# First pair's key norm moved up a tile, six low parts given to GpSimd, the first gates' sigmoid ahead of a copy

## The reference, cut to what matters

```python
z = h @ w_in                                        # h = rmsnorm(x)
kk = heads(kf * k_k)                                # k is a slice of z
kk = kk / maximum(sqrt(sum(kk * kk, -1)), 1e-12)    # the key norm
S = S * w_t + (S @ -kk) (kk * a)^T + v k^T          # the scan over tokens
y = (groupnorm(y) + bonus) * g
g_a, g_b = split(sigmoid(z_gate + gate_b), 2)
x = x + (g_a * (y @ w_proj_a) + g_b * (attn @ w_proj_b)) @ w_out
x = x + conv_ffn(rmsnorm(x))
```

## Time and profile before

| | |
|---|---|
| median of 3 runs | 1123.92 us (1123.31 to 1125.4) |
| the profiled execution, its own time | 1125.01 us |
| its span (first to last instruction) | 1123.0 us |
| PE busy | 1095.9 us, 98% of the span |
| DVE busy | 687.6 us, 61% |
| ACT busy | 503.7 us, 45% |
| POOL busy | 92.8 us, 8% |
| PE share of the chain that ended last | 88%; DVE 7%, ACT 1% |
| granted TensorE clock | 0.999 |

### The profile page before, as it was taken

The page is one execution under the profiler, slowest core; times in us unless marked ns, Lnnn a source line. Parts: engine busy times, 40 slices in busy tenths (PEclk is TensorE's granted clock), DMA queues, the critical chain, the costliest instruction groups (busy, mean ns, idle before and its releaser), DMA issues.

```text
span 1123.0 us, 17984 instructions
## 1 busy us (share of the span) xinstructions
PE 1095.9 (98%) x6760; PEld 864.9 (77%) x6760; DVE 687.6 (61%) x1163; ACT 503.7 (45%) x865; POOL 92.8 (8%) x145
## 2 busy tenths in 40 slices
PE   7999999989999999999999999999999999999997
PEld 6887888767777777777766888888888888888886
DVE  4224566678878777787785444547776777752224
ACT  6426555633524445253533333455556555641122
POOL 8100001101010110101110100100000000000000
PEclk9999999999999999999999999999999999999999
DMA  8632333210111111111312544333332333232221
GB/s 212 131 94 76 94 95 94 76 39 20 39 39 48 39 57 57 48 58 39 113 57 86 153 137 131 123 103 103 93 95 83 105 93 97 86 105 94 94 75 75
DMA packets 154390, 97.01 MB, mean 86 GB/s; under 512 B 30761, under 2 KB 143575, under 8 KB 154327
## 3 DMA queue, kind: packets, MB, share of 16 engines
q1 hardware_dynamic: 148800, 79.72, 24.5%
q0 software_dynamic: 5376, 16.37, 4.6%
q10 hardware_dynamic: 151, 0.04, 0.0%
HBM read 87.71 MB, written 8.39 MB: 86 GB/s over the span
## 4 chain that ended last, share of the span: by engine, by line
PE 88%; DVE 7%; ACT 1%; DMA 1%; issue 1%; SPq 1%; DVEq 0%; ACTq 0%
PE ps L1607 15%; PE ps L1610 15%; PE ps L1609 15%; PE ps L1590 5%; PE ps L2086 4%; PE ps L2087 4%; PE ps L2085 4%; PE ps L1592 4%; PE ps L1591 4%; PE ps L1734 3%; PE ps L1884 2%; PE ps L1863 1%; PE ps L1688 1%; PE ps L1819 1%; PE ps L1682 1%; DMA raw<-in_w_in 1%
## 5 line engine op out<-in xcount | busy, mean ns | idle before, releaser
L1096 DVE TENSOR_TENSOR wlo<-raw,whi 128x1024 fp32r<-128x1024 f32 x142 | 173.5, 1222 | 214.2 <-ACT whi L691 141.7
L691 ACT ACTIVATE whi<-raw 128x1024 fp32r<-128x1024 f32 x124 | 131.1, 1057 | 133.1 <-PE ps L1610 124.5
L1607 PE MATMUL ps<-xnh,whi 128*128 128x512 f32 x344 | 136.0, 395 | 0.0
L1610 PE MATMUL ps<-xnh,wlo 128*128 128x512 f32 x344 | 135.9, 395 | 0.0
L1609 PE MATMUL ps<-xnl,whi 128*128 128x512 f32 x344 | 135.9, 395 | 0.0
L1607 PE MATMUL ps<-xh,whi 128*128 128x512 f32 x248 | 99.7, 402 | 3.0 <-DVE xl L1114 1.7
L1610 PE MATMUL ps<-xh,wlo 128*128 128x512 f32 x248 | 97.9, 395 | 0.0
L1609 PE MATMUL ps<-xl,whi 128*128 128x512 f32 x248 | 97.8, 394 | 0.0
L1590 PE MATMUL ps<-xh,whi 128*128 128x512 f32 x184 | 88.6, 481 | 0.0
L1610 PEld LDWEIGHTS ps<-xnh,wlo 128*128 128x128 f32 x344 | 64.6, 188 | 15.8
L1607 PEld LDWEIGHTS ps<-xnh,whi 128*128 128x128 f32 x344 | 64.6, 188 | 15.6
(11 more groups left out here) (335 smaller groups left out, 2211.8 us busy)
## 6 DMA issues: line engine op xcount, KB each, us to landing
raw<-in_w_in SPq DMA_DIRECT2D x108, 256.0 KB, 3.2
raw<-in_w_up SPq DMA_DIRECT2D x88, 256.0 KB, 3.1
raw<-in_w_down SPq DMA_DIRECT2D x44, 256.0 KB, 2.8
gates_scratch<-gst POOLq DMA_DIRECT2D x16, 256.0 KB, 2.4
raw<-in_w_proj_b SPq DMA_DIRECT2D x16, 256.0 KB, 4.0
raw<-in_w_proj_a SPq DMA_DIRECT2D x16, 256.0 KB, 3.0
gl<-gates_scratch POOLq DMA_DIRECT2D x16, 256.0 KB, 3.1
raw<-in_w_out SPq DMA_DIRECT2D x16, 256.0 KB, 3.0
```

Source lines behind the costliest of these rows:

```text
L691: act.activation(flat(whi[:, hb]), flat(raw[:, b]), ACT.Copy).then_inc(w_hi, 1)
L1096: dve.tensor_tensor(flat(lo[:, hb]), flat(raw[:, b]), flat(hi[:, hb]).bitcast(F32), ALU.subtract).then_inc(w_lo, 1)
L1607: pe.matmul(ps[bank][:, :], whi[:, hb, k, :], hi(k), start=first and k == 0, stop=False)
L1610: ins = pe.matmul(ps[bank][:, :], wlo[:, hb, k, :], hi(k), start=False, stop=last and k == kn - 1)
```

## The change

Three things are changed.

1. For pair 0, PE's `key_sums` and `small_products` move from ahead of tile 15 to the middle of tile 14 (ahead of step k = 4), and PE's `key_norms` from ahead of tile 16 to the middle of tile 15 (ahead of k = 4). ACT's `key_norm_back` moves ahead of `rkv(15)`. ACT's `key_norm`, `decay_tanh` and `rate_tanh` stay where they were, behind the copies of tile 14 and of the last attention chunk.
2. Six low parts of 128x1024 (three `ybl`, three `yal`) go from DVE to POOL. POOL makes the first three behind the last pair's `remainder`, the other three behind the last `attention_back` and ahead of `gates_back`. A new semaphore `yl_pool` counts them.
3. On ACT the first gates' sigmoid goes ahead of the split of weights `N_PROJ + 2`, in which ACT waits for PE, and of the last `yah` copy. On DVE the split of the same weights goes ahead of the last `yal` part.

```diff
+            def y_lo(dst, src, hi, i, order):
+                pool.wait_ge(yh_ready, order + 1)
+                pool.tensor_tensor(flat(dst[:, 2 * i:2 * i + 2]), flat(src[:, 2 * i:2 * i + 2]),
+                                   flat(hi[:, 2 * i:2 * i + 2]).bitcast(F32), ALU.subtract)\
+                    .then_inc(yl_pool, 1)
...
                 remainder(n)
+                if n == PAIRS - 1:
+                    for i in range(3):
+                        y_lo(ybl, qb, ybh, i, i)
...
             attention_back(3)
+            for i in range(3):
+                y_lo(yal, z, yah, i, 3 + i)
...
                     rate_tanh(0, 4)
+                    key_norm_back(0, 2)
                 if t == RKV_TILES - 1:
-                    key_norm_back(0, 2)
                     exponentials_of(0)
...
             deviation(PAIRS - 1)
+            act.wait_ge(gate_in[0], 32)
+            act.activation(flat(gs[:, 0]), flat(gl[:, 0]), ACT.Sigmoid).then_inc(gate_ready, 1)
             weights(N_PROJ + 2)
...
-                    if lv >= 4 and not following:
-                        y_lo(1, lv - 4, lv - 4)
...
             scan(PAIRS - 1, [lambda: weights(N_PROJ + 1), lambda: add_bonus(PAIRS - 1),
-                             lambda: y_lo(0, 0, 3), lambda: y_lo(0, 1, 4), lambda: y_lo(0, 2, 5),
                              lambda: y_lo_of(flat(ybl[:, 6:8]), flat(q67), flat(ybh[:, 6:8]), 6),
                              lambda: y_lo_of(yal[:, 6, :], z[:, 6, :], yah[:, 6, :], 7)])
...
+            weights(N_PROJ + 2)
             y_lo_of(yal[:, 7, :], z[:, 7, :], yah[:, 7, :], 8)
-            weights(N_PROJ + 2)
...
+            def first_norm(k):
+
+                if k == 8 * (RKV_TILES - 3) + 4:
+                    pe.wait_ge(consts, 3)
+                    pe.wait_ge(misc_in, 16 * 11)
+                    pe.wait_ge(vtok_ready, 8)
+                    pe.wait_ge(sc_ready, 8)
+                    key_sums(0, 2)
+                    small_products(0, (3, 4))
+                if k == 8 * (RKV_TILES - 2) + 4:
+                    key_norms(0, 2)
```

More of the change, by code:

```diff
@@ L361, in build @@
         yl_ready = sem("yl_ready")
+        yl_pool = sem("yl_pool")
         mix_ready = sem("mix_ready")
@@ L1001, in projections @@
                     n, m = i * 4 + N_PROJ + u, i * 2 + u // 2
-                    if u % 2 == 0:
+                    if u % 2 == 0 and (u or not first):
                         act.wait_ge(gate_in[u // 2], i * 32 + 32)
@@ L1375, in scan @@
                     piece()
[L1377 to L1381, removed]
             def rkv(t):
@@ L1934, in __call__ @@
                         if self.t == 23:
-                            pe.wait_ge(yl_ready, self.tile.k // 2 + 1)
+                            pe.wait_ge(yl_pool, self.tile.k // 2 + 1)
                         self.tile(1)
@@ L1972, in _ @@
                         values(c + 1)
[L1973 to L1981, removed]
+                product(n, t % 2, t % 2, xs(xh), xs(xl), tile_n=n,
+                        ready=lambda k: first_norm(8 * t + k))
             pe.wait_ge(o_done, 8)
@@ L2000, in _ @@
             gate(PAIRS - 1, 3)
-            pe.wait_ge(yl_ready, 3)
+            pe.wait_ge(yl_pool, 3)
             scan(PAIRS - 1, lambda place: tb(1 if place == (1, "state") else 0))
@@ L2004, in _ @@
             norm_var(PAIRS - 1)
-            pe.wait_ge(yl_ready, 4)
+            pe.wait_ge(yl_pool, 4)
             tta(2)
             deviations(PAIRS - 1)
-            pe.wait_ge(yl_ready, 7)
+            pe.wait_ge(yl_ready, 1)
             tb(2)
+            pe.wait_ge(yl_pool, 6)
             tta(4)
             for k in range(2):
-                pe.wait_ge(yl_ready, 8 + k)
+                pe.wait_ge(yl_ready, 2 + k)
                 tta(1)
```

## The result

| | before | after |
|---|---|---|
| median of 6 runs each | 1124.28 us | 1134.7 us (1132.44 to 1139.99) |
| the profiled execution | 1125.01 us | 1133.88 us |
| its span | 1123.0 us | 1131.9 us |
| granted TensorE clock, mean | 0.999 | 0.993 |

The ratio after to before is 1.0098, with a 95% interval of 1.0079 to 1.0117. The kernel became slower by 10.4 us. The forecast was +3.9, with a range of 1124.8 to 1133.0, so its sign was right, and the time lies above the range.

A forecast was written before the change was run, and what follows sets the result against it. PE was taken as the bound, busy 98% of the span, so only its idle stretches could change. +2.07 - 1.7 + 2.2 + 2.1 - 0.8 = +3.9 us on the median 1123.92 gave 1127.8 us; range 1124.8 to 1133.0.

The forecast's parts named there:

- Part 1: Pair 0's key norm: longer tile 14 delays ACT, PE idles 1.66 in tile 15, scores start later: +2.07 us.
- lower bound of 0.41: Pair 0's key norm: if the norm came in time, only its turn on PE would remain, costing 0.41 us.
- Part 2, the gain: Last inverse: two subtractions leaving DVE shorten PE's two waits for the masked product, 1.8 together: -1.7 us.
- Place one: Last inverse: POOL's subtractions and DVE's two-SBUF-input `wlo` and `xx` block each other in turns, delaying PE: +2.2 us.
- Place two: Last scan: `wlo` held 0.1 to 0.2, then POOL's subtractions hold `ybl` and half `yal` in turns: +2.1 us.
- third rival: POOL keeps its turn through three subtractions: last inverse 4.7, last scan 4.5; +8.8, 1132.7 us, chance 0.16.
- Part 3: Before the third projection tile: sigmoid moved into ACT's idle time removes PE's wait for `ta`: -0.8 us.

The follow-up runs named there:

- part 1 alone: Kernel before with only pair 0's key sums, small products, key norms and norm copy-back at their new places: 1125.73 us, ratio 1.0017.
- part 2 alone: Kernel before with only the six low-part subtractions (three `ybl`, three `yal`) moved from DVE to POOL: 1131.21 us, ratio 1.0062.

## Why the prediction was right and wrong

- **Part 1: right.** Forecast: an idle of 1.66 for `kqn` and scores 2.07 later. Measured: 1.56 (1.55 alone) and 2.20 (2.19 alone). Two things in it were wrong without showing in the sum. The lower bound of 0.41 overlooked a second path, ACT's chain to DVE, which has a floor of 0.99. And behind the idle of 1.56 and the 2.17 ahead of the scores the clock fell in the profiled execution of after, though not in that of part 1 alone.
- **Part 2, the gain: right.** The waits for `v` in the last inverse fell from 1.8 to 0.2 (over the kernel from 3.0 to 1.3). Forecast: 1.7; measured where nothing is held: 2.0.
- **Place one, the last inverse: the mechanism right, the size about right.** `wlo` took 1.67 (forecast over 1.5), `xx` 2.87 (over 2.5), PE idled 1.49 and 0.30. The net of this place and the gain was +0.1 (30.86 - 30.73) where the forecast had +0.5. Against 28.70, the same stretch with the `ybl` on POOL and nothing held, the hold cost 2.2, as forecast. It is only +0.1 with the clock at full: in three of the six profiled executions with this hold the clock fell behind it, which costs another 1.5 to 1.6. No term had that.
- **Place two, the last scan: the step that failed.** The forecast said that `wlo` is held 0.1 to 0.2 and that the block comes in turns, later, at `ybl` and the half `yal`: +2.1. In its place `wlo` stood through all three subtractions (5.93), as the third rival had it, but at this place only. The term of that rival for it was 4.5. The traces give 4.0: from the first `zp` to the last `up` 12.05 us before, and 611.78 - 595.76 = 16.02 with the clock at full.
- **A term that was missing: PE's clock.** The same stretch is 19.55 in after, so the half clock cost 3.5 there, and 1.65 in the front of the profiled execution. Together with the block, place two cost 7.5 where the forecast had 2.1. No rival had the clock. The prediction counted PE's idle time as idle time and no more. Turns like those that it forecast at place two brought the clock down too, in the kernel that took them, and cost 4.6 there instead of 2.1. The Trainium skill, "TensorE: Matmul & The Clock Gate", section "Part 1: The HAM clock gate", says that an idle engine is at 1.2 GHz. For the wait of 5.12 us the traces agree (0.50 in 602 to 610); the falls behind shorter waits are known here from the traces alone.
- **Part 3: right in the trace** (the wait of 0.8 is gone), too small for the runs to tell.

The corrected sum in the profiled executions: +2.2 (part 1), +0.1 (place one with the gain), +4.0 (block at place two), +3.5 and +1.65 (clock), -1.5 (the sigmoid's 0.8 and 0.7 without a name), -1.1 (the start): 8.9. The sigmoid's 0.8 can't be read off the stretch at the end: from the last `up` on, part 2 alone takes 517.6 us, and the two kernels with a memset or a DMA more, which don't differ from it behind this point, take 520.1. By runs alone the parts give +1.4 to +1.9, +7.0 and -0.5 to -0.1, some 8 to 9 of the 10.4. The rest is within the intervals, and more half clock may be in it, in the front and in the last inverse. In how many executions it occurs at each place stays open; the mean clocks of 0.985 and 0.988 in the two slowest runs say that some have more of it than the profiled one.

Why did I choose wrongly at place two? The evidence lay in one row: DVE's `t<-t` began at 218.37, before POOL's memset at 218.86, and ended behind it. I held against it the rule of the Trainium skill, "SBUF — State Buffer", section "Who interferes with whom", that "issue order, not op shape, decides who blocks". The row was right. That memset too stands right behind a DMA of POOL, at 218.10 in the trace of before, as the three `yal` do. The place that took turns has no DMA ahead. (Whether the DMA is what let the memset keep `t<-t` out was not tried: the kernel that moved the memset took it out of DVE's way as a whole.) Between two rows that disagree I should have looked for what differs in front of them.

## What to carry to other kernels

Work given to GpSimd is not free because GpSimd is idle: list every DVE instruction with two SBUF inputs within its time, and don't leave out instructions like `t<-t`, which has one and took 2.68 us beside a memset. See what GpSimd does just ahead, since a DMA issue there turned three subtractions into one block of 7 us. A wait of TensorE costs more than its length once it brings the clock down, so price an idle stretch of 5 us at 8 to 9, and many small waits aren't safe either. Where a wait can't be avoided, idle matmuls in it are worth trying, and where an offload fits, a start bound to the moment at which the other engine leaves its two-input instructions makes the gain real.

## What the runs showed of the hardware

- A float32 subtraction of 128x1024 takes 2.32 us on POOL (6.96 for three) and 1.22 on DVE.
- Without a DMA ahead, POOL and DVE alternate, one instruction each (`wlo` 1.67, `xx` 2.87 in after). Behind a DMA that POOL issued within 0.6 us before them, three POOL instructions in a row made one DVE instruction of 1.22 us take 5.93, 5.94, 5.99 and 5.99 us in the last scan of four kernels, and 6.90 and 5.93 at the two places of a fifth. A tiny memset and a wait behind the DMA (1.49), or waits between the three instructions (1.35), restored the turns. Why a DMA has this effect, the runs don't tell.
- The clock was at half for some 10 us around the end of an idle stretch of 5.12 us and behind it (601 to 611 in after). It also fell behind three waits of 0.53, 1.09 and 1.59 us, behind 1.56 and 2.17 us, and behind 1.49 and 0.30 us, but with either of the last two patterns only in some of the profiled executions. 64 idle transposes in the waits kept it at full in the front part and in the last scan, not in the last inverse, where none stood, and brought 4.0 us.
